# Neighbourhood and sliding attention turned by transposes, with the scaling of the rows moved to ScalarE and VectorE

## What is computed

```python
def _neighbourhood_attention(...):        # first block, 8 heads of 64
    s_loc = q_r . k_b + bias              # 256 keys of the grid window, with relative bias, masked
    s_ctx = q_r . k_ctx                   # all 256 context keys
    p = softmax(concat(s_loc, s_ctx))
    o = p_loc . v_b + p_ctx . v_ctx

def swa_with_sinks(q, k, v, sinks):       # second block, 16 query heads of 64, window 128
    m = maximum(max(logits), sink)
    pexp = exp(logits - m)
    probs = pexp / (sum(pexp) + exp(sink - m))
    out = probs . v                       # 256 keys a block of 128 queries, 128 in block 0
```

## Time and profile before

| | us |
|---|---|
| median of 3 runs | 2887.65 |
| lowest, highest | 2886.82, 2888.18 |
| the profiled execution, its own time | 2887.88 |
| its span, first to last instruction | 2886.1 |
| mean granted TensorE clock | 0.995 |

### The profile page before, as it was taken

One profiled execution on the slowest core, in us unless ns is written; L12 is line 12 of the kernel. 1 busy time (PEld: TensorE's weight loads), 2 busy tenths in 40 slices (PEclk: granted clock), 3 DMA queues, 4 the chain that ended last, 5 costly groups with the idle time before them and its releaser, 6 DMA issues.

```text
span 2886.1 us, 29737 instructions
## 1 busy us (share of the span) xinstructions
PE 2822.2 (98%) x11810; PEld 2027.2 (70%) x11810; DVE 1355.1 (47%) x2510; ACT 492.5 (17%) x1075; POOL 793.0 (27%) x668
## 2 busy tenths in 40 slices
PE   8999999999999999999999999999999999999997
PEld 3655555555887367866888886775558867888873
DVE  7666565567117454325332336217554325544443
ACT  2100000003016153113000002005340001000011
POOL 1233343331312002411444430110014412444420
PEclk9999999999999999999999999999999999999999
DMA  6334333331100101221222221220102222222211
GB/s 244 120 106 131 98 117 121 95 135 70 64 25 1 45 15 48 85 95 49 96 86 86 85 82 59 77 72 16 43 31 88 88 95 73 88 88 88 88 58 59
DMA packets 51753, 231.66 MB, mean 80 GB/s; under 512 B 4256, under 2 KB 10784, under 8 KB 38176
## 3 DMA queue, kind: packets, MB, share of 16 engines
q1 hardware_dynamic: 40960, 181.17, 18.2%
q0 software_dynamic: 9072, 39.85, 4.3%
q10 hardware_dynamic: 1584, 8.75, 0.8%
HBM read 227.66 MB, written 2.10 MB: 80 GB/s over the span
## 4 chain that ended last, share of the span: by engine, by line
PE 58%; DVE 2%; ACT 0%; issue 0%; DVEq 0%; ACTq 0%
PE banks L649 39%; PE banks L585 14%; PE banks L762 1%; PE banks L1225 1%; PE banks L594 1%; DVE scratch_a L2345 0%; PE banks L1150 0%; PE banks L1134 0%; PE banks L1227 0%; PE banks L1232 0%; DVE rstd L1757 0%; PE banks L1203 0%; PE banks L601 0%; DVE normed L1760 0%; DVE bias_mask L2362 0%
## 5 line engine op out<-in xcount | busy, mean ns | idle before, releaser
L649 PE MATMUL banks<-big 128*128 128x256 f32 (+1 forms) x2240 | 572.2, 403 | 0.0
L2485 POOL TENSOR_TENSOR big<-weight_ring 128x512 f32<-128x512 f32 (+2 forms) x117 | 141.4, 1209 | 1409.3 <-PE banks L649 746.0
L649 PEld LDWEIGHTS banks<-big 128*128 128x128 f32 x2240 | 424.9, 190 | 112.8 <-DVE rpb_rows L1876 2.5
L649 PE MATMUL banks<-big,weight_ring 128*128 128x256 f32 (+1 forms) x1504 | 398.2, 409 | 3.4 <-DVE scratch_a L1882 2.6
L649 PEld LDWEIGHTS banks<-big,weight_ring 128*128 128x128 f32 x1504 | 285.3, 190 | 87.8 <-DVE scratch_a L1882 3.8
L649 PE MATMUL banks<-normed,weight_ring 128*128 128x256 f32 (+1 forms) x1312 | 342.6, 404 | 2.1 <-ACT rstd L1689 1.3
L585 PE MATMUL banks<-normed,weight_ring 128*128 128x256 f32 (+4 forms) x944 | 305.1, 481 | 1.2 <-ACT normed L1315 0.6
L649 PEld LDWEIGHTS banks<-normed,weight_ring 128*128 128x128 f32 x1312 | 249.1, 190 | 69.6 <-ACT rstd L1689 2.1
L585 PEld LDWEIGHTS banks<-normed,weight_ring 128*128 128x128 f32 (+2 forms) x944 | 176.0, 188 | 122.2 <-issue 106.6
L2486 POOL TENSOR_TENSOR big<-weight_ring 128x512 f32<-128x512 f32 (+2 forms) x142 | 211.6, 1490 | 0.0
L649 PE MATMUL banks<-normed,big 128*128 128x256 f32 (+1 forms) x840 | 203.7, 389 | 0.0
(11 more groups left out here) (428 smaller groups left out, 3408.0 us busy)
## 6 DMA issues: line engine op xcount, KB each, us to landing
weight_ring<-weights SPq DMA_DIRECT2D x144, 1024.0 KB, 4.8
rpb_rows<-w_ada POOLq DMA_DIRECT2D x28, 512.0 KB, 3.9
p_embed<-w_ada POOLq DMA_DIRECT2D x28, 512.0 KB, 3.8
weight_ring<-weights SPq DMA_DIRECT2D x16, 768.0 KB, 4.3
weight_ring<-weights SPq DMA_DIRECT2D x14, 512.0 KB, 3.5
weight_ring<-weights SPq DMA_DIRECT2D x8, 640.0 KB, 3.7
big<-w_ada POOLq DMA_DIRECT2D x2, 2048.0 KB, 8.4
residual<-xT ACTq DMA_DIRECT2D x2, 1536.0 KB, 12.2
```

Source lines behind the costliest of these rows:

```text
L649: last = nc.tensor.matmul(z, stationary(p), moving(p), start=opens and p == 0, stop=p == kp - 1, skip_group_check=True)
L2485: T(w[2], a11, a21, ALU.subtract).then_inc(sums_c, 1)
```

## The change

In both attentions the turn becomes a transpose against the plain identity, so the rows must be scaled before it.

- Neighbourhood: `DIAG` and `diagonal` go. VectorE only takes the reciprocal (`na_inverse`, with a signal of its own, "inverse"); ScalarE scales the 512-wide rows in place, one unit behind its exponentials, and gives the "norm" signal. The copy of the turned unit from PSUM moves from ScalarE to VectorE (`na_turned`), between maxima and reciprocal.
- Sliding: `scaled_turn` goes. VectorE scales the rows of each head in place (256 columns, 128 in block 0) in place of the identity's 128 columns. The reduction of `sw_maxima` starts from the negated sink, a column, in place of a constant, and the separate minimum goes. The wait on the turns for a free `DIAG` goes.
- An unused signal of the merges goes.

```diff
-                            last = nc.tensor.matmul(bank[:, 2 + u % 2, c * P:(c + 1) * P],
-                                                    NA_ROWS[:, u % 6, c * P:(c + 1) * P], DIAG[:, u % 4, :],
-                                                    start=True, stop=True)
+                            last = nc.tensor.transpose(bank[:, 2 + u % 2, c * P:(c + 1) * P],
+                                                       NA_ROWS[:, u % 6, c * P:(c + 1) * P], ident)
...
-                return [[(SQ5[:, u % 3, (2 * e + c) * P:(2 * e + c + 1) * P], DIAG[:, 2 * (u % 2) + e, :])
+                return [[SQ5[:, u % 3, (2 * e + c) * P:(2 * e + c + 1) * P]
                          for c in range(1 if blk == 0 else 0, 2) for e in range(2)]]
...
-            attention(asw, 32, sw_scores, sw_pieces, scaled_turn, sw_values, asw["max"], (4, 5), 2, 4, 1)
+            attention(asw, 32, sw_scores, sw_pieces, transposed, sw_values, asw["max"], (4, 5), 2, 4, 1)
...
-            for i in range(NA_HEADS * N_BLK + 4):
+            for i in range(NA_HEADS * N_BLK + 1):
                 if i < NA_HEADS * N_BLK:
                     act.wait_ge(ana["max"], i + 1)
                     A(NA_ROWS[:, i % 6, :], NA_ROWS[:, i % 6, :], ACT.Exp, bias=stat_col(i, 0), scale=-1.0,
                       accum_out=stat_col(i, 2)).then_inc(ana["exp"], 1)
-                if i >= 4:
-                    u = i - 4
-                    if u >= 4:
-                        act.wait_ge(ana["pv"], u // 2 - 1)
-                    act.wait_ge(ana["t"], u + 1)
-                    A(NA_TURNED[:, u % 4, :], bank[:, 2 + u % 2, :], ACT.Copy).then_inc(ana["tc"], 1)
+                if i >= 1:
+                    u = i - 1
+                    act.wait_ge(ana["inverse"], u + 1)
+                    A(NA_ROWS[:, u % 6, :], NA_ROWS[:, u % 6, :], ACT.Copy,
+                      scale=stat_col(u, 3)).then_inc(ana["norm"], 1)
...
-            def diagonal(g, u, turned):
-
-                dve.wait_ge(g["exp"], u + 1)
-                link(V.reciprocal(stat_col(u, 3), stat_col(u, 2)))
-                if turned > 0:
-                    dve.wait_ge(g["t"], turned)
-                V.tensor_scalar(DIAG[:, u % 4, :], ident, stat_col(u, 3), None, ALU.mult).then_inc(g["norm"], 1)
...
+            def na_turned(u):
+                if u >= 4:
+                    dve.wait_ge(ana["pv"], u // 2 - 1)
+                dve.wait_ge(ana["t"], u + 1)
+                V.tensor_copy(NA_TURNED[:, u % 4, :], bank[:, 2 + u % 2, :]).then_inc(ana["tc"], 1)
+
+            def na_inverse(u):
+                dve.wait_ge(ana["exp"], u + 1)
+                V.reciprocal(stat_col(u, 3), stat_col(u, 2)).then_inc(ana["inverse"], 1)
...
+                if 4 <= i < NA_HEADS * N_BLK + 4:
+                    na_turned(i - 4)
                 if 1 <= i <= NA_HEADS * N_BLK:
-                    diagonal(ana, i - 1, i - 4)
+                    na_inverse(i - 1)
...
-                                                 con("sw_mask", lo, 256 - lo), -1.0, -BIG_NEG, ALU.add, ALU.min,
-                                                 stat_col(u, 8 + e))
+                                                 con("sw_mask", lo, 256 - lo), -1.0,
+                                                 nsink[:, 2 * pair + e:2 * pair + e + 1], ALU.add, ALU.min,
+                                                 stat_col(u, e))
                     if e == 0:
                         mark(ins)
                 link(ins)
-                link(V.tensor_tensor(stat_col(u, 0, 2), stat_col(u, 8, 2), nsink[:, 2 * pair:2 * pair + 2], ALU.min))
...
-                if u >= 2:
-                    dve.wait_ge(asw["t"], u - 1)
                 for e in range(2):
-                    ins = V.tensor_scalar(DIAG[:, 2 * (u % 2) + e, :], ident, stat_col(u, 10 + e), None, ALU.mult)
+                    p = SQ5[:, u % 3, e * 256 + lo:(e + 1) * 256]
+                    ins = V.tensor_scalar(p, p, stat_col(u, 10 + e), None, ALU.mult)
```

More of the change, by code:

```diff
@@ L294, in build @@
         NA_BIAS = view(p_sb, 0, 2, 512)
-        DIAG = view(bm_t, 0, 4, P)
         def mla_turned(u):
@@ L433, in build @@
         vt = st("vt", "done", "act", "dve")
-        ana = st("att_na", "s", "bias", "max", "exp", "norm", "t", "tc", "pv", "oc")
+        ana = st("att_na", "s", "bias", "max", "exp", "inverse", "norm", "t", "tc", "pv", "oc")
         amla = st("att_mla", "s", "max", "exp", "norm", "t", "tc", "pv", "oc")
@@ L438, in build @@
         gen = st("mla_gen", "kr", "kr_roped", "q", "qc", "rot", "q_roped", "k", "kc", "v", "vc")
-        mrg1, mrg2 = stages(2, "merge", "done", "gate", "free")
+        mrg1, mrg2 = stages(2, "merge", "gate", "free")
         ple = st("ple", "done", "gate", "free")
@@ L759, in transposed @@
                 return nc.tensor.transpose(at, rows, ident)
-            def scaled_turn(at, pair):
-                return nc.tensor.matmul(at, pair[0], pair[1], start=True, stop=True)
             def attention(g, units, scores, pieces, turn, values, s_freed, t_banks, o_banks, per_out, together):
@@ L2355, in sw_normalise @@
             def sw_normalise(u):
+                lo = P if u % 4 == 0 else 0
                 dve.wait_ge(asw["biased"], u + 1)
```

## The result

The changed kernel took 2867.83 us as the median of four runs (2866.34 to 2868.95), the kernel before 2887.66: a ratio of 0.9932 [0.992, 0.9943], 19.8 us less. The forecast was 2866.2, 21.4 less.

A forecast was written before the change was run, and what follows sets the result against it. TensorE, busy for 98% of the span, was taken to bound the kernel. Neighbourhood 14.5 plus sliding 6.9 made 21.4 us off, a median of 2866.2 us; own range 2864 to 2869, wider range 2862 to 2874.

The forecast's parts named there:

- The turns: Both attentions: a transpose costs one TensorE record, a product two, so each turned 128x128 block saves 0.109 us.
- Neighbourhood attention: First stage: TensorE stays the bound, a pair goes from 4.07 to 3.20 us; 14.5 us saved, bounds 13.0 and 15.5.
- ScalarE's scaling: Neighbourhood rows, 128x512 within SBUF: priced at 0.57 us like a square, upper bound the exponential's 0.72.
- Sliding attention: Second stage: a group of four units goes from 9.21 to 8.35 us; 6.9 us saved, bounds 1.8 and 14.
- the ring: Sliding attention: maxima, exponentials, eviction, values, scores; a two-unit lap of 4.26 us, hidden under TensorE, becomes 4.06 and sets the pace.
- I take nothing, since it already writes its result to such a column: Sliding reduction: extra cost of a column as start value set at nothing; at most 0.16 us, twice a lap.
- the maxima of line 2345: Sliding attention, a sign of being wrong: these maxima growing beyond 0.42 us.
- a clock under 1.00 beyond a few microseconds: Either attention stage, a sign of being wrong: TensorE's granted clock standing under 1.00 that long.
- the rival's two steps: Both attention stages: thinned TensorE work lowers the clock, low half the time, 12 us more than before, 2900; chance 0.06.
- VectorE's copy did not wait for GpSimd: Neighbourhood attention, rival denied here: the copy held up 0.5 us, a pair needs 4.0, kernel 2880.7 us; chance 0.04.
- Sliding attention gives nothing: Rival: seeding costs as much as the removed operation and the take falls wholly on the ring; 2873 us, chance 0.12.
- falls to VectorE's own work: Sliding attention, rival: only VectorE's busy time is left, 7.4 us a group, kernel 2859 us; chance 0.06.

The follow-up runs named there:

- e1: The kernel before with only the neighbourhood part of the diff, sliding attention as before: 2872.29 us, ratio 0.9944.
- e7: The kernel before with the sliding scores of the next unit issued ahead of the values, not behind them: 2887.67 us, ratio 1.0.
- e6: The changed kernel with the sliding scores of the next unit issued ahead of the values, not behind them: 2866.35 us, ratio 0.9923.
- e3: The changed kernel with the sliding reduction's constant start and the separate minimum with the sink put back: 2869.45 us, ratio 0.9936.
- e0: The changed kernel run once more, unaltered, as a base: 2867.65 us.
- e8: The changed kernel with one 256-column product of constants ahead of each of the first four sliding units' scores: 2866.11 us.
- e5: The changed kernel with neighbourhood rows scaled by VectorE within SBUF and the turned unit's eviction back on ScalarE: 2878.61 us, ratio 0.9966.

## Why the prediction was right

**The turns.** One record fewer for each block, 240 in all: as forecast. The priced 0.109 was a little low: 0.96 less a pair, 0.12 for each of 8 records. Records alone stand 0.11 apart; the rest around a run of turns also shrank, from about 0.24 to 0.15. What that rest is was not looked into.

**Neighbourhood attention, 14.5 forecast, 15.3 measured** (e1 alone the same, 15.7 by its median). The sum 16 x 0.96 = 15.4 comes so near by two things that cancel: until the third pair's turns the stage saves 2.5 us, 0.5 beyond the two pairs' own, as forecast; from the turns of the last but one pair on, where no scores are left in between and TensorE waits a little for VectorE's copies, it saves 0.6 less than its share, which the forecast did not have. TensorE stayed the bound, and VectorE waits 0.42 before the maxima, where 0.3 was forecast. ScalarE's scaling came at the upper bound of its price: 0.707 as a median, not the 0.57 of a square. It did no harm because 0.35 us a pair were left idle there.

**Sliding attention, 6.9 forecast, 5.7 measured.** The mechanism was right where it counted: the ring, not the limit before (e7), sets the pace after (e6). That TensorE's work alone had hidden it was not quite so: a wait for VectorE of 0.51 stood in one round of four. The mis-sized term is the one marked unknown, "I take nothing, since it already writes its result to such a column". It costs 0.06 for each reduction, and the lap is 4.19 in place of 4.06, the group 8.51 in place of 8.35: 8 x 0.16 = 1.3 us, the whole of the miss. That the maxima of line 2345 would grow beyond 0.42 was named as a sign of being wrong, and they did, to 0.48. The change's seeding is still worth its place, about 1.6 us (e3; 8 x 0.21 by the groups), not the 3.2 of 0.20 twice a group.

**The clock.** Said to make the prediction wrong was also a clock under 1.00 beyond a few microseconds. It was 0.50 for 7 us in one profiled execution and 10 in the other, against 3.4 before, at the start of the sliding stage and never in a steady lap (in e0 once more, for 3.4 us, as the stage drained). So this sign came true too, and the forecast survived it because it cost only 1 to 3 us (71.24 and 73.73 for the stage, against 70.52 in e8). The fall comes in the kernel before as in the changed one, behind the same thin start (1.63 us busy of 4), so the change did not start it. That thinner work behind it lengthens it is likely and not shown: of the four unfilled profiled executions whose sliding turns are products, two had 3.4 us and two 6.8; of the six with transposes, one had 6.8 and five 10.2. The first stage is not safe either: it ran at 1.00 in both profiles of the changed kernel, but the clock fell for 3.4 us there in e7, whose first stage is that of the kernel before, and for 6.8 in e5.

Of the rival's two steps the fall was real, its spread over half of both stages was not. By the rule of the Trainium skill that the prediction weighed ("TensorE: Matmul & The Clock Gate", Part 4: PE-mode transpose), as the prediction read it, the stages would have stayed low. They hold a quarter of transposes (128 of 512 records, 112 of 464); the first ran at 1.00 throughout, the second did so once its start was filled. Work of transposes alone was seen only for the 4.5 us of line 904 (40 of the 42 records of that row; the other two are products), behind a long stretch of products, so it doesn't settle the rule.

**The sum.** 15.3 + 5.7 + 0.5 = 21.5 between the profiled executions; the medians differ by 19.8. Most of the 1.7 between them is that the changed kernel's profiled execution is the lowest of its four, 1.5 below their median. Three of the four had the same mean clock, 0.994, the lowest and the highest among them, so the record does not show low stretches as the reason. That the forecast came within 2 us of the time is in part luck: the first stage gave 0.8 more than its term and the second 1.2 less.

**The other rivals.** VectorE's copy did not wait for GpSimd (0.687 as a median of 32; on why, see e5). That rival named a real mechanism, though, at the wrong operation: the same engine's scaling within SBUF doubles there, and e5 shows what the other split of the work would have cost, 11 us. "Sliding attention gives nothing" fell; "falls to VectorE's own work" holds only once the ring is cut, at 7.99.

## What to carry to other kernels

When an engine's work is thinned, price the ring that it had hidden, lap by lap, and then the engine behind that: here the group lay at 9.21, 8.51 and 7.99 us with three different bounds, and only moving one thing in the order of issue, with a look at the waits that were left, told them apart. Before an operation is moved, look at which memory it reads, who works beside it and who begins first: a copy out of PSUM kept its 0.69 us beside GpSimd, a scaling within SBUF, begun just behind GpSimd's sum, went from 0.49 to 0.98. A stage that opens with TensorE half idle can cost microseconds of low clock later on; four products on constants kept it at 1.00, for some 2 us by the medians in the changed kernels and for nothing in the one before. The first of them put the stage off by 0.60; ahead of the wait it might have cost nothing, which was not tried. And count a stage from its first extra instruction, not from its first useful one.

## What the runs showed of the hardware that had not been expected

- ScalarE's copy with a column as scale, 128x512 within SBUF, took 0.707 us, like an exponential (0.72) and not like a square (0.57).
- VectorE's masked reduction takes 0.06 us more with a column as its start value than with a constant, at 128 columns (0.342 against 0.282) and at 256 (0.478 against 0.419).
- VectorE's scaling within SBUF, begun behind a GpSimd sum of 0.73 us, ended 1.01 us behind the sum's start whether it began 0.03 or 0.31 behind it (0.98 and 0.70 long), and took 0.49 with no sum beside it.
- The low clock at one place of one program lasted 7 us in one execution and 10 in another, and stretches of 3.4 us came behind it in some executions and not in others.
